# Second MLP of a two-block sequence model: seven quadrant products in place of eight for five of its eight down chunks

## What is computed

```
hdn = square(relu(x @ w1))        # x 1024 x 1024, w1 1024 x 4096
y   = hdn @ w2                    # w2 4096 x 1024
h   = layer_norm(ALPHA * x + y)
```

## Time and profile before

| what | value |
| --- | --- |
| median of 3 runs | 2749.52 us (2747.79 to 2753.2) |
| profiled execution, its time | 2750.66 us |
| its span in the profile | 2748.9 us |
| PE busy | 2591.2 us, 94% of the span, 13052 matmuls |
| DVE busy | 1533.6 us, 56% |
| ACT busy | 1064.7 us, 39% |
| POOL busy | 846.6 us, 31% |
| mean granted clock of PE | 0.974 of full speed |

### The profile page before, as it was taken

One profiled execution on the slowest core, in us unless ns is written; L12 is line 12 of the kernel. 1 busy time (PEld: TensorE's weight loads), 2 busy tenths in 40 slices (PEclk: granted clock), 3 DMA queues, 4 the chain that ended last, 5 costly groups with the idle time before them and its releaser, 6 DMA issues.

```text
span 2748.9 us, 33651 instructions
## 1 busy us (share of the span) xinstructions
PE 2591.2 (94%) x13052; PEld 1342.9 (49%) x13052; DVE 1533.6 (56%) x2452; ACT 1064.7 (39%) x1318; POOL 846.6 (31%) x557
## 2 busy tenths in 40 slices
PE   6999999887999999999979899888999999999998
PEld 3677666543444444444454444344544444444443
DVE  6255353567745556555585739764335746444435
ACT  3434324124544343434254254243434533434441
POOL 1211122113344454441641322116111233333332
PEclk9999999998999999999989999999999999999999
DMA  7321130301112212221021221010010111111121
GB/s 304 109 76 62 51 123 31 108 31 35 31 62 73 73 58 89 69 81 46 32 92 47 92 93 57 10 67 31 31 46 31 62 46 62 47 62 47 46 77 62
DMA packets 71168, 182.51 MB, mean 66 GB/s; under 512 B 6080, under 2 KB 12640, under 8 KB 64224
## 3 DMA queue, kind: packets, MB, share of 16 engines
q1 hardware_dynamic: 55328, 138.89, 14.9%
q10 hardware_dynamic: 15680, 41.46, 4.4%
HBM read 170.90 MB, written 9.45 MB: 66 GB/s over the span
## 4 chain that ended last, share of the span: by engine, by line
PE 79%; DVE 9%; ACT 4%; DVEq 3%; issue 2%; POOLq 1%; DMA 1%; ACTq 1%; POOL 1%; SPq 0%
PE PS L790 23%; PE PS L791 23%; PE PS L792 23%; DVE XT L2356 1%; PE PS L829 1%; PE PS L1576 1%; DVEq L2355 1%; PE PS L1549 1%; ACT WB L1643 1%; ACT WS L1645 1%; PE PS L1078 1%; DMA Hf<-in_w_ada 1%; POOLq L718 1%; POOLq L716 1%; PE PS L1045 1%
## 5 line engine op out<-in xcount | busy, mean ns | idle before, releaser
L635 POOL TENSOR_TENSOR WB<-WS,WB 128x512 f16<-128x512 f32 x208 | 257.9, 1273 | 1008.4 <-ACT WS L1645 1008.4
L790 PE MATMUL PS<-WB,Hf 128*128 128x512 f16 x1440 | 550.6, 382 | 15.1 <-DVE Hf L2356 5.1
L791 PE MATMUL PS<-WB,Hf 128*128 128x512 f16 x1440 | 549.8, 382 | 0.0
L792 PE MATMUL PS<-WB,Hf 128*128 128x512 f16 x1440 | 549.6, 382 | 0.0
L790 PE MATMUL PS<-XT,WB 128*128 128x512 f16 x1088 | 416.7, 383 | 15.0 <-DVE Hf L2354 9.7
L791 PE MATMUL PS<-XT,WB 128*128 128x512 f16 x1088 | 416.5, 383 | 0.0
L792 PE MATMUL PS<-XT,WB 128*128 128x512 f16 x1088 | 415.9, 382 | 0.0
L2713 DVE SCALAR_TENSOR_TENSOR R<-PS,R 128x512 f32<-128x512 f32 x320 | 220.5, 691 | 266.3 <-PE PS L792 249.2
L660 POOL TENSOR_TENSOR WB<-WS,WB 128x1024 f16<-128x1024 f32 x84 | 189.6, 2257 | 375.6 <-ACT WB L1933 204.9
L649 POOL TENSOR_TENSOR WB<-WS,WB 128x512 f16<-128x512 f32 x128 | 163.9, 1310 | 250.7 <-ACT WS L1645 249.0
L790 PEld LDWEIGHTS PS<-WB,Hf 128*128 128x128 f16 x1440 | 142.0, 99 | 190.6 <-issue 11.6
(11 more groups left out here) (406 smaller groups left out, 3903.2 us busy)
## 6 DMA issues: line engine op xcount, KB each, us to landing
WS<-in_w_ff SPq DMA_DIRECT2D x32, 1024.0 KB, 5.2
WS<-in_mlp_w SPq DMA_DIRECT2D x32, 1024.0 KB, 5.1
WS<-in_w_mix SPq DMA_DIRECT2D x20, 1024.0 KB, 4.8
Hf<-in_w_ada ACTq DMA_DIRECT2D x12, 1024.0 KB, 5.9
Hf<-in_w_ada SPq DMA_DIRECT2D x8, 1024.0 KB, 10.8
WS<-in_w_out SPq DMA_DIRECT2D x8, 1024.0 KB, 5.1
R<-in_x SPq DMA_DIRECT2D x4, 1024.0 KB, 9.7
R<-in_x ACTq DMA_DIRECT2D x2, 2048.0 KB, 7.8
```

The source lines that it names most:

```text
L635: op = pool.tensor_tensor(WB[:, slot, 1, at:at + n], WS[:, hf, i * n:(i + 1) * n], WB[:, slot, 0, at:at + n], ALU.subtract)
L790: pe.matmul(o, ah, bh, start=(first and k == 0), stop=False, skip_group_check=True)
L791: pe.matmul(o, ah, bl, start=False, stop=False, skip_group_check=True)
L792: mm = pe.matmul(o, al, bh, start=False, stop=(last and k == n - 1), skip_group_check=True)
```

## The change

For the second MLP, the down work of chunks 2 to 6 is also made of seven quadrant products; the down work of chunks 0, 1 and 7 keeps its eight, from quadrants. The hidden chunk is cut in four blocks (token half by half of the 512 hidden columns: a11, a12, a21, a22) and the weight chunk in four quadrants of 256 x 512.

- PE: a product is four jobs of 6 matmuls, in the order q21 by a12, q11 by a11, t2 by s2, t3 by s3, t4 by a22, t1 by s1, q22 by s4. Four of them (`first` False) go on accumulating in the banks that the product before left. Product t4 of the up work runs after the first down product.
- DVE: 28 additions to R for such a chunk in place of 16; four sums of the down weights (`stream_sums`); four sums of the hidden blocks, each of two instructions (`row_sum`); a remainder for each of seven activation forms, each of two instructions (`row_lo`).
- ACT: the high parts of all weight forms; the high parts of the seven activation forms (`row_hi`), which DVE's rounding made before.
- POOL: seven forms of 1024 elements for such a down chunk in place of eight pieces of 512. Both staging halves are given free together, after the seventh form.
- Weight forms lie in a ring of eight places in WB, activation forms in a ring of seven places in H; which place a form gets, and the job that must be done before, is worked out by `weight_places` and `row_places` when the program is built.

```
+        DOWN_PRODUCTS = (("q21", "a12", 0, 0, True), ("q11", "a11", 0, 0, True), ("t2", "s2", 0, 1, False),
+                         ("t3", "s3", 1, 1, False), ("t4", "a22", 1, 0, False), ("t1", "s1", 1, 1, True),
+                         ("q22", "s4", 0, 1, False))
+        WEIGHT_FORMS = ("q11", "q21", "q22", "t1", "t2", "t3", "t4")
+        ROW_FORMS = ("a12", "a11", "a22", "s1", "s3", "s2", "s4")
```

PE's down product, and POOL's remainders of a chunk:

```
+                def down_product(u, i):
+                    form, rows, _, _, first = DOWN_PRODUCTS[i]
+                    pe.wait_ge(form_lo, 7 * form_base("D", u) + FORM_INDEX[form] + 1)
+                    pe.wait_ge(h_lo, 7 * (u - 2) + ROW_FORMS.index(rows) + 1)
+                    for t in range(4):
+                        b = wide_bank()
+                        gemm(PS[:, b, :], lambda k: tuple(row_form(u, rows, l)[:, k, t * P:(t + 1) * P] for l in range(2)),
+                             lambda k: tuple(weight_form("D", u, form, l)[:, k, :] for l in range(2)), 2,
+                             first=first).then_inc(job_done, 1)
+                        J[0] += 1
...
+            def stream_forms(kind, u):
+                base = form_base(kind, u)
+                for form in FORM_INDEX:
+                    pool.wait_ge(form_hi, 6 * base + (1 if kind == "D" and form == "q21" else FORM_HI[form]))
+                    pool.tensor_tensor(weight_form(kind, u, form, 1), weight_stage(kind, form),
+                                       weight_form(kind, u, form, 0), ALU.subtract)
+                    pool.drain().then_inc(form_lo, 1)
+                pool.sem_inc(w_stage_free, 2)
```

ACT's queue in a turn u, x the down chunk u-1 and y the next up chunk:

```
+                    for u in range(2, NF):
+                        at, x = FAST_BASE[m] + u - 2, ("D", u - 1)
+                        y = ("U", u + 1) if u < NF - 1 else ("D", NF - 1)
...
+                        if u - 1 in FAST_DOWN:
+                            row_hi(u - 1, "s2")
+                            row_hi(u - 1, "s4")
+                        for f in range(2):
+                            keep(0, f, f)
+                        stream_half(*x, 0)
+                        squares(0)
+                        stream_half(*x, 1)
+                        for f in range(2):
+                            keep(1, 4 + f, f)
+                        stream_sum(*x, 1)
+                        for f in range(2):
+                            keep(0, 6 + f, f)
+                        stream_sum(*x, 2)
+                        squares(1)
+                        stream_sum(*x, 3)
+                        squares(2)
+                        stream_sum(*x, 4)
+                        row_hi(u, "a12")
+                        stream_half(*y, 0)
+                        last_squares(u)
+                        row_hi(u, "a11")
+                        stream_half(*y, 1)
+                        row_hi(u, "a22")
+                        stream_sum(*y, 1)
+                        if u in FAST_DOWN:
+                            row_hi(u, "s1")
...
+                        stream_sum(*y, 2)
+                        if u in FAST_DOWN and u > 2:
+                            row_hi(u, "s3")
+                        stream_sum(*y, 3)
+                        stream_sum(*y, 4)
```

DVE's queue in a turn u:

```
+                    for u in range(1, NF):
+                        if u > 1:
+                            if u - 1 in FAST_DOWN:
+                                row_sum(u - 1, "s2")
+                                row_lo(u - 1, "s3")
+                                row_sum(u - 1, "s4")
+                                row_lo(u - 1, "s2")
+                                row_lo(u - 1, "s4")
+                            for n in range(6):
+                                tile_sum(u, n)
+                                if u - 1 in FAST_DOWN and n in (1, 3, 5):
+                                    stream_sums("D", u - 1, {1: ("t1", "t2"), 3: ("t3",), 5: ("t4",)}[n])
+                        if u - 1 in FAST_DOWN:
+                            rows = {1: ("a12",), 2: ("a11",), 3: ("a22",)}
+                            for i in range(7):
+                                down_sums(u - 1, i)
+                                if i == 2 and u < NF - 1:
+                                    stream_sums("U", u + 1, ("t1",))
+                                for name in rows.get(i, ()):
+                                    row_lo(u, name)
+                                if i in (4, 5, 6) and u < NF - 1:
+                                    stream_sums("U", u + 1, ("t%d" % (i - 2),))
...
+                                if i in (4, 5):
+                                    row_sum(u, ("s1", "s3")[i - 4])
+                                if i == 6:
+                                    row_lo(u, "s1")
```

More of the change, by code:

```diff
@@ new lines, in weight_places @@
+        def weight_places():
+            uses, places = stream_uses(), {}
+            free = [((u, 8, 0), 4 * ((C["mlp2"] + u) % 2) + i, (job_done, WIDE["mlp2"] + 8 * u + 8))
+                    for u in range(2) for i in range(4)]
+            chunks = [("D", 0)] + [x for u in range(2, NF) for x in (("U", u), ("D", u - 1))] + [("D", NF - 1)]
+            for kind, u in chunks:
+                for form in forms_of(kind, u):
+                    free.sort(key=lambda x: x[0])
+                    _, at, ready = free.pop(0)
+                    places[kind, u, form] = at, ready
+                for form in forms_of(kind, u):
+                    key, ready = uses[kind, u, form]
+                    free.append((key, places[kind, u, form][0], ready))
+            return places
@@ L1210, in mlp @@
                 chunk_used()
+                if last:
+                    second_stream(q0)
+                    return
                 for u in range(1, NF):
@@ L2047, in mlp @@
                 hidden(0, None if last else s5_setup)
-                for u in range(1, NF):
+                if last:
+                    hidden(1)
+                    second_stream()
+                for u in range(1, NF) if not last else ():
                     if u in fast:
@@ L2059, in mlp @@
                     J[0] += 16
[L2060 to L2062 removed]
                 if not last:
+                    for hf in range(2):
+                        round_down(NF - 1, hf)
+                    J[0] += 16
                     s5_turn(7)
@@ L2851, in corners, with stream_sums @@
                         corner_remainders(k)
+                def stream_sums(kind, u, forms):
+                    base = form_base(kind, u)
+                    for form in forms:
+                        if form == "t1":
+                            dve.wait_ge(form_hi, 6 * base + (1 if kind == "U" else 2))
+                        else:
+                            dve.wait_ge(form_lo, 7 * base + 4)
+                        out, a, b = {"t1": ("q12", "q12", "q11"), "t2": ("q22", "q22", "t1"), "t3": ("q11", "t2", "q11"),
+                                     "t4": ("q21", "q21", "t2")}[form]
+                        dve.drain()
+                        dve.tensor_tensor(weight_stage(kind, out), weight_stage(kind, a), weight_stage(kind, b),
+                                          ALU.subtract).then_inc(form_sum, 1)
@@ new lines, in tile_sum @@
+                def tile_sum(u, n):
+                    at, f, name = FAST_BASE[m] + u - 2, n % 2, ("a11", "a12", "a22")[n // 2]
+                    bank, i, job, copy = ((6, 0, 2, 1), (4, 0, 8, 5), (6, 1, 10, 3))[n // 2]
+                    dve.wait_ge(up_kept, 6 * at + copy + f)
+                    dve.wait_ge(up_done, 14 * at + job + f + 1)
+                    dve.drain()
+                    dve.tensor_tensor(row_tile(u, name, f), as_tile(PS[:, bank + f, :], name), as_tile(kept(m, i, f), name),
+                                      ALU.add).then_inc(up_sum, 1)
@@ new lines, in row_lo @@
+                def row_lo(u, name):
+                    place = PLACE_OF.get(name, name)
+                    names = ROW_FORMS if u in FAST_DOWN else ROW_BLOCKS
+                    dve.wait_ge(h_hi, 7 * (u - 2) + names.index(name) + 1)
+                    for f in range(2):
+                        op = dve.tensor_tensor(as_tile(row_form(u, name, 1)[:, f, :], place), row_tile(u, place, f),
+                                               as_tile(row_form(u, name, 0)[:, f, :], place), ALU.subtract)
+                    op.then_inc(h_lo, 1)
@@ L2867, in down @@
                                 columns_half(0, XT)
-                for u in range(NF):
+                for u in range(2 if last else NF):
                     if u in fast:
```

268 lines of the change are left out of this document (259 added, 9 removed).

## The result

The changed kernel takes 2779.1 us, against 2749.5 for the kernel before on the same chip: a ratio of 1.0107 with a 95% interval of 1.009 to 1.0125. It is 29.6 us slower. The prediction had the sign and missed the size: it said 7.4 us, and its range ended at 2767.

A forecast was written before the change was run, and what follows sets the result against it. PE was taken as the bound. Turns 4 to 7 were put at 72.5 + 5.4 (chain) + 1.5 (clock) + 1.0 (banks) = 80.4 us against 77.7, +11.3; with turn 3's -3.9, +7.4 on 2749.5 gave 2757 us, range 2727 to 2767.

The forecast's parts named there:

- POOL in DVE's way: DVE instructions with both operands in SBUF wait for a running POOL instruction, 0 to 2.1 us per collision; sign: weight sums' mean over 2 us.
- The chain to the first copy: DVE's queue from A to ACT's first copy of the next turn, ending at A + 26; PE waits 5.4 us with signals.
- point A: The moment PE ends down product five of seven, with two products, 10.4 us, left; the chain is counted from it.
- step (2): In DVE's queue: sum t2 of the next up chunk and `row_sum` s1, 2.7 us, ending at A + 3.8.
- step (6): In DVE's queue: four additions, 3.0 us, ending at A + 14.0, 3.6 behind PE.
- step (9): In DVE's queue, the next turn's part: `row_sum` s2, which meets POOL's t4, 2.1 + 1.35 us.
- step (11): In DVE's queue: `row_sum` s4, 1.35 us, ending at A + 24.1, before ACT casts s4 and makes the copy.
- The banks: Down part: `row_lo` a22 meets three POOL instructions, and additions of products five and seven may free banks late; 1.0 us taken.
- The clock: After PE's wait for the copy, matmuls restart at a granted clock of 0.53; 1.5 us a turn in turns 4 to 7.
- Turn 3: After a down of full products, the copy comes in time, 8.9 us into the turn; saves 5.2, loses 1.3: -3.9 us.
- all of the gain: Rival: DVE meets POOL nowhere that counts, the chain ends 0.4 us late; -24.3 us, 2725 us; chance 0.13.
- The worse case: Rival: DVE's collisions with POOL's back-to-back instructions cost another 1.5 us per turn, 2763 us; chance 0.45 together with the forecast.

The follow-up runs named there:

- e3: The changed kernel with POOL filling the remainders of the second MLP's seven-product weight forms with zeros, not subtracting, these remainders left out of the computation; 2729.8 us, ratio 0.9916.
- e6: The changed kernel with DVE's remainders of a12 and sum t1 of the next up chunk each one product earlier in the down part; ratio 1.0059.
- e4: The kernel before, with eleven copies of a tile onto itself on ACT ahead of the first copy out of PSUM in six turns; 2795.3 us, ratio 1.0155.
- e7: The changed kernel with the sixteen additions of a row to the residual moved from DVE's down part of turn 2 to turn 1; ratio 1.0065.
- e13: e11 with ACT's cast of a11 ahead of the up chunk's first half and DVE's remainders of a11 behind product two; 2745.7 us, ratio 0.9981.
- e11: e9 with DVE's tile sums of a22 ahead of down sums t3 and t4, and sum t1 of the next chunk behind product three; ratio 1.0003.
- e14: e13 with POOL filling the remainders of the seven-product forms with zeros, these remainders left out of the computation; ratio 0.9921.
- e9: The changed kernel with several reorderings of ACT's and DVE's queues combined, and ACT's other four copies out of PSUM in a turn made early too; ratio 1.0037.
- e10: The changed kernel with ACT's order of e9 alone, DVE's queue as it was; ratio 1.0028.

## Why the prediction was wrong in size

**What bounds the kernel:** right. PE without a gap, at 0.216 us per matmul, and the others with slack by their shares.

**What is removed:** right, 120 matmuls, 25.9 us. e3 shows that 22.8 of it are there to be had.

**POOL in DVE's way:** right, and shown by e3. The sign named for it, weight sums with a mean over 2 us, was not seen: their mean is 1.79, against 1.83 before. What the collisions cost lies in single places, such as the 5.14 us above, and the mean hides them.

**The chain to the first copy:** right in its members and their order, each of which stands in the rows above. It was sized 5.4 us and measured 3.77 in turns 4 to 7. Counted from the prediction's point A in turn 4 (2472.7), step (2) ended at A + 3.6 for 3.8, step (6) at A + 13.5 for 14.0, step (9) at A + 20.3 for 21.4, step (11) at A + 22.9 for 24.1, and the first copy at A + 24.5 for 26: no step was far off, and together they came out 1.5 us shorter. That PE is held back just before, and so asks later, plays a smaller part at most: in e6 it is held back by 0.5 us in turn 3, and the wait for the copy behind it is 4.43.

**The banks:** this is the first failed term, "0 to 2 us, I take 1.0". It measured 3.7 to 4.0 us in each of turns 3 to 6. The prediction had the remainders of a22 meet POOL's three instructions in a row; those take 1.28 us (DVE, at 2467.98), and it is the remainders of a11, one product earlier, that meet them. Nor did it count that each of a pair can lose a POOL instruction: 5.14 us for 1.3 of work. Chain and banks together measured 7.5 us, against 6.4.

**The clock:** the second. It was priced at 1.5 us once a turn, from an idle stretch in another part of the kernel. It falls behind both waits of a turn, and each fall costs about 2: 4 to 5 us per turn in place of 1.5. e4 gives the price by itself. It is the largest part of what was missed in turns 4 to 6, some 3 us of the 4.2 to 4.6 by which these turns are longer than forecast.

**Turn 3:** the third, and a step rather than a size: "DVE has 2.6 us per job and ends level with PE". The sixteen residual additions, which the change leaves in turn 2, share it now with two `row_sum` and four `row_lo`, of which one pair of each kind meets POOL (5.15 and 4.97 us). DVE's last addition of turn 2 ends at 2323.2, 12.4 us after PE has begun turn 3, PE waited 7.67 us where none was forecast, and lost about 2 more to the clock; with the bank wait and its fall of the clock the turn came out 13.7 us above its forecast. That is more than half of the 24.4 us by which the span missed. e7 takes the wait away, and the turn is 9.2 us shorter.

**The sum** itself has a small slip: by its own terms turns 4 to 7 give 4 x 2.7 = 10.8, not 11.3, and the banks stand at 1.3 in turn 3 and at 1.0 in the others. Nothing hangs on it.

**The rivals:** "all of the gain" at 2725 is what a kernel without the collisions does (2729.8), so its arithmetic held and its condition did not. The worse case added 1.5 us per turn where 4.2 to 4.6 were missing in three turns and 13.7 in one; turn 7 came out 2.3 shorter than forecast. The range was too narrow above because every unknown cost was bounded by one collision or one fall at a time, and none was counted a second time.

## What to carry to other kernels

Where PE is full, an engine's busy share says little; follow the queue of the engine that must answer, instruction by instruction, up to the point at which PE asks, and count a collision of DVE and POOL for each instruction and not for each group when POOL runs back to back. Price a wait of PE of over 3.5 us at its length plus 1.3 to 2 us or a little more, each time; for one of about 2 to 3.3 us allow for the fall or for none. Whoever adds work to DVE in such a loop should place its instructions with two SBUF operands where POOL is idle, and the ones that read PSUM where it is busy; most orders tried here that took one wait away made another.

## What the runs showed of the hardware that was not expected

A shorter wait may cost no clock at all, and its length alone does not say whether. In e13 the granted clock, in the four microseconds behind each wait, is 0.58 behind 3.18 us and 1.00 behind 2.92 and 2.05 us:

```profile
2453.00:2457.00 4.00, 4.00 (x12) 1.48 (x12) 3.63 (x5) 0.00 (x0) 0.97 (x1) 0.58 0.01 2
2530.20:2534.20 4.00, 4.00 (x19) 1.85 (x20) 3.63 (x5) 0.00 (x0) 1.06 (x1) 1.00 0.00 0
2683.60:2687.60 4.00, 4.00 (x19) 1.81 (x20) 3.72 (x6) 0.00 (x0) 1.16 (x2) 1.00 0.00 0
```

But the clock is 0.58 behind a wait of 2.02 us in e7 and 1.00 behind one of 3.34 us in e11:

```profile
2457.60:2461.60 4.00, 3.98 (x11) 1.49 (x12) 3.82 (x5) 0.00 (x0) 3.21 (x2) 0.58 0.00 0
2600.90:2604.90 4.00, 4.00 (x19) 1.85 (x20) 3.81 (x5) 2.28 (x4) 3.45 (x2) 1.00 0.02 4
```

Over the turns 2 to 7 of the changed kernel and of all the experiments but e3 and e14, the clock fell behind each of the 48 waits of 3.56 us and more, behind 19 of the 36 from 1.93 to 3.34 us, and behind none of the 91 up to 1.61 us. What decides between 1.93 and 3.34 us stays open. It bears on e9 and e10: with 28.1 and 27.0 us of waits, e10 is 4 us faster, and the clock falls behind one of its waits and behind four of e9's. This is a reading of the rows and not tested by itself.

And a pair of short DVE instructions beside a busy POOL can take four times its own length, 5.14 us for 1.3, which no row of the kernel before had shown.
